# Value pages of a paged attention cache in 2 KB pieces on every eighth partition, two page groups to a double slot

## The chip, the cores and the metric

The kernel runs on one core of a Trainium2 chip. The time is device microseconds of one execution; the times given are those of several runs, and the profile is one more execution, taken by the hardware profiler.

## The reference: what is computed

One decoder layer for two request groups that share all weights: a prompt of 256 tokens, and 8 sequences of 8 new tokens each (64 rows) with 2,048 cached positions behind them. Model width is 1,024, so 320 rows go through everything: a SwiGLU feed-forward (width 2,816), a mixer, a second SwiGLU feed-forward, each with a layer norm behind it and scales and shifts from a condition vector.

The mixer has an attention half (8 heads of 64) and a convolution half (512 channels, 31 taps). For the 8 sequences the attention reads a paged cache. A page holds 128 positions of all 8 heads, as (head, position, 64) in float32: 256 KB of keys and 256 KB of values. Each sequence has 16 pages, in the order of a page table; together they are 32 MB of keys and 32 MB of values. Two pages make a block of 256 positions. Each query picks the three blocks of eight whose key sums score highest, and the softmax runs over those blocks and the new tokens, with a penalty per head that grows with distance. All pages are read, and blocks that were not picked are masked:

```
scores = q . k * scale - slope[head] * (q_pos - k_pos)      (all 2,048 positions)
gate   = q . mean(k of a block)      ->  the 3 highest blocks of 8
p      = softmax over picked blocks and own new tokens
out    = sum over positions of p * v
```

## The kernel before, in words

All five engines have their own hand-written instruction stream, tied by semaphores. SP issues nearly all loads in one fixed order; ACT issues a few of them. The order of the program is: feed-forward 1, the input projection of the mixer, the cached attention, the output projection, feed-forward 2. The weights are loaded in pieces of 1 KB per partition and row (`cols`), 1 MB at a time. At the very start SP also loads the tokens into `xrow`: `x_prompt` as 4 KB pieces on all 128 partitions (1 MB, line 484), and right behind it `x_sample` as 4 KB pieces on partitions 0 to 63 (256 KB, line 485).

**Chunks, slots, order.** The cached attention works on four pairs of sequences, j = 0 to 3. A pair has 32 pages. Four pages form a chunk of 1 MB, so a pair has eight key chunks and eight value chunks (k = 0 to 7; k 0 to 3 are the first sequence's, 4 to 7 the second's). The 64 chunks have numbers, `kvi`, and are loaded in this order: keys of pair 0, keys 1, values 0, keys 2, values 1, keys 3, values 2, values 3. They land in a ring of eight slots (`kv_slot`), each 128 partitions by 2,048 floats. The slots lie two by two: slots 0 to 3 are the tensor `raw`, 4 and 5 are `araw`, 6 and 7 are `kvw`. A chunk may be loaded when the chunk before it in its slot is used up (`kv_before`; the loop over `kvi` in the SP block). For keys this is the semaphore `kt_ready` (both halves turned), for values it is `v_used`. The last eight value chunks take slots 0 to 5, 2 and 3, since `kvw` takes the first two parts of the output weights `w_out` by then; SP issues those two loads behind value chunk 3 of pair 3, once the last two value chunks of pair 2 are used.

**How a page lands.** `load_pages` issues one DMA per page, four per chunk (x = 0 to 3). A key page covers all 128 partitions with 2 KB each. A value page x goes to partitions x, x + 4, x + 8 and so on, 32 of them, and on each come eight pieces of 1 KB (one per head, four positions each). The four pages of a chunk together fill all 128 partitions of one slot. For pairs 0 to 2 SP issues the pages x = 0, 1, 2 of each value chunk, and ACT issues x = 3 (`last_page` in `keys_low`), between its copies of the next pair's keys. For pair 3 SP issues all four.

**Keys.** For each key chunk PE turns the pages with 16 transposes (`turn_keys`, line 1865), ACT copies one half out of PSUM to `kT` (line 973) and DVE the other (line 1369), and PE multiplies with the queries (`scores`, line 1890). DVE then adds the distance term and takes sums and maxima per block (`score_chunk`).

**Values.** `pair_probs` turns the softmax numerators. `pair_values` (line 1960) takes chunk after chunk: it waits until the chunk has landed (`raw_wait`), does 8 products with the turned numerators as weights, and raises `v_used` by 1. The small steps of the next pair's softmax (`gate_sum`, `max_swap`, `prob_sum`), and in the last pairs those of the group norm and of the output projection, are called between chunks by the table `between`. Value chunks of pair j - 1 are used after the keys of pair j.

Of the kernel before, what the change touches and what calls it, by code (L numbers as in the profile page):

```python
# [72 lines left out]
def constants():  # L73
# [12 lines left out]

    col = np.arange(P)
    wide = np.arange(4 * P)
    c[:, C_POS:C_POS + 4 * P] = (wide // P % 2 * P + wide % P // 4 * 4 + 2 * (wide // 256))[None, :]

    h, r, t = p // 16, p // 8 % 2, p % 8
    m = 2.0 ** (-(h + 1.0))
# [152 lines left out]
def build(nc, i, o):  # L245
    es = ExitStack()
    with es:
# [96 lines left out]
        def kv_raw(kvi):  # L344

            k = kv_slot(kvi)
            return raw[:, k, :] if k < RING else (araw, kvw)[k // 2 - 2][:, k % 2, :]

        def kT_view(k, half):

            return kT[:, k % 2, 1024 * half:1024 * half + 1024].rearrange("p (x n q) -> p x q n", x=4, q=2)

        def bank_keys(half):

# [83 lines left out]
        def load_pages(eng, cache, kvi, page, xs=range(4)):  # L438

            slot = kv_raw(kvi)  # L440
            for x in xs:
                src = i["cache_" + cache][0][bass.ds(page[2 * x], 1)]
                if cache == "k":
                    eng.dma_start(slot[:, 512 * x:512 * x + 512], src.rearrange("a h (g r) d -> (a h g) (r d)", r=8)).then_inc(kv_in[kv_slot(kvi)], 16)
                else:
                    eng.dma_start(slot[x:P:4, :].rearrange("p (h f) -> p h f", h=NH),
                                  src.rearrange("a h (g r) d -> g (a h) (r d)", r=4)).then_inc(kv_in[kv_slot(kvi)], 16)


        @block.sync  # L450
        def _(sp):
# [98 lines left out]
            for kvi in range(KVN):  # L550
# [2 lines left out]
                    store_keys()  # L553
                if k % 4 == 0:
                    numbers = page_numbers(2 * j + k // 4)
                before = kv_before(kvi)
                if before is not None:
                    cache_b, jb, kb = kv_chunk(before)
                    sp.wait_ge(*((kt_ready, 2 * (8 * jb + kb + 1)) if cache_b == "k" else (v_used, 8 * jb + kb + 1)))
# [132 lines left out]
        def _(act):  # L692
# [264 lines left out]
            def keys_low(j, between={}):  # L957

                def last_page(k, page):

                    kvi = values_at(j - 1, k)
                    act.wait_ge(kt_ready, 2 * (8 * j + k + 1))
                    load_pages(act, "v", kvi, page[8 * (k % 4 // 2) + k % 2:], range(3, 4))

                numbers = None
                for k in range(8):
                    n = 8 * j + k
                    if j and k % 4 == 1:
                        numbers = page_numbers(2 * (j - 1) + k // 4, mybir.EngineType.Activation)
                    act.wait_ge(kt_ready, 2 * n + 1)  # L970
                    if n >= 2:
                        act.wait_ge(k_used, n - 1)
                    act.copy(kT_view(k, 0), bank_keys(0)).then_inc(kt_low, 1)  # L973
                    if n in ACT_HIGH:
                        act.wait_ge(kt_ready, 2 * n + 2)
                        act.wait_ge(kt_high, n)
                        act.copy(kT_view(k, 1), bank_keys(1)).then_inc(kt_high, 1)
                    if j and k:
                        last_page(k - 1, numbers)
                    if k in between:  # L980
                        between[k]()
                if j:
                    last_page(7, numbers)
# [549 lines left out]
        def _(pe):  # L1533
# [334 lines left out]
            def scores(j, k):  # L1868
# [9 lines left out]
                if k % 2 == 0:  # L1878
# [3 lines left out]
                        pe.wait_ge(s_evac, g + 3)  # L1882
                    elif j:
                        pe.wait_ge(pt_evac, 5 * j)
                keys = kT[:, k % 2, :].rearrange("p (i x h n) -> p i x h n", i=2, x=4, h=NH)
                for e in range(2):
                    for g4 in range(NHP):
                        h = 2 * g4 + e
                        out = bank[QG * g4:QG * g4 + QG, 4 + g % 2, :].rearrange("p (i c n x) -> p i c x n", i=2, c=2, x=4)[:, :, k % 2]
                        ins = pe.matmul(out, qb[:, 2 * j + k // 4, h, :], keys[:, :, :, h, :], start=e == 0, stop=e == 1)  # L1890
                ins.then_inc(k_used, 1)

# [37 lines left out]
            def pair_probs(j):  # L1930
# [4 lines left out]
                for r in range(4):  # L1935
                    if r >= 2:
                        pe.wait_ge(pt_evac, 5 * j + r - 1)
                    for x in range(4):
                        at = 512 * (r % 2) + 256 * (x % 2) + 128 * (x // 2)
                        ins = pe.transpose(bank[:, 4 + r % 2, P * x:P * x + P], s[:, r // 2, at:at + P], ident)  # L1940
                    ins.then_inc(pt_ready, 1)
                pe.wait_ge(ri_ready, j + 1)
# [4 lines left out]
            def pair_values(j, between):  # L1947


                if j:  # L1950
                    pe.wait_ge(av_evac, j)
                for k in range(8):
                    c, b2 = k % 4, k // 4
                    kvi = values_at(j, k)
                    raw_wait(kvi)
                    values = kv_raw(kvi).rearrange("p (h f) -> p h f", h=NH)
                    for i_ in range(2):
                        at = P * (8 * b2 + 2 * c + i_)
                        for g4 in range(NHP):
                            ins = pe.matmul(bank[QG * g4:QG * g4 + QG, 7, 256 * b2:256 * b2 + 256].rearrange("p (e f) -> p e f", e=2),  # L1960
                                            pT[:, at + QG * g4:at + QG * g4 + QG], values[:, 2 * g4:2 * g4 + 2, P * i_:P * i_ + P],
                                            start=(c == 0 and i_ == 0), stop=False)
                    ins.then_inc(v_used, 1)
                    if k in between:
                        between[k]()
                    if c == 3:

                        for g4 in range(NHP):
                            diagonal = bank[QG * g4:QG * g4 + QG, 7, 256 * b2:256 * b2 + 256].rearrange("p (a d) -> p a d", a=4)[:, 0:4:3, :]
# [65 lines left out]
                products(first[2 * u:2 * u + 2], m_parts(MIX_ORDER[c0:c1]), lambda n: pe.wait_ge(ml_ready, 16 + c0 + n + 1),  # L2035
                         start=c0 == 0, stop=False)

            pair_values(3, {2: group_scales, 5: lambda: conv_half(0, 0, NCC), 6: lambda: conv_half(1, 0, 2)})
            conv_half(1, 2, 3)
            attn_turn(3)  # L2040
            conv_half(1, 3, NCC)
# [74 lines left out]
```

## Time and profile before

| | |
|---|---|
| median of 3 runs | 912.44 us (907.31 to 916.94) |
| the profiled execution | 915.39 us |
| its span in the trace | 913.6 us |
| its mean granted clock of TensorE | 0.968 |
| PE busy | 848.8 us (93%) |
| DVE / ACT / POOL busy | 457.4 / 352.0 / 269.3 us |
| data moved by DMA | 197.44 MB, 216 GB/s over the span |
| chain that ended last | PE 73%, DVE 9%, DMA 6%, ACT 5% |

PE is the busiest engine over the whole program, since the three feed-forward and projection stages are nearly all PE. The cached attention is another stage with other limits. It lies between 430 and 628 us of the span: keys of pair 0 from 430, keys 1 from 458, values 0 from 492, keys 2 from 509, values 1 from 540, keys 3 from 558, values 2 from 583, values 3 from 603 to 627. Busy shares of the whole span say little about it; the rows below are of that stage.

The column for DMA in the windows view is the mean busy share of the 16 DMA engines, and can exceed 1 a little because packets overlap. Times of a load are from its issue to its landing.

### The profile page before, as it was taken

The page shows a single profiled execution, that of the slowest core. Times are in us where ns is not written, and L with a number is a line of the kernel's source. Part 1 is how long each engine was busy: PE and PEld are TensorE (multiplying, and loading weights), DVE is VectorE, ACT ScalarE, POOL GpSimd, SP SyncE. Part 2 cuts the span into 40 slices and gives each one's busy share as a digit, 9 for nine tenths or more (in the row PEclk, how much of TensorE's full clock was granted, in tenths as well). Part 3 has the DMA queues.
Part 4 walks back from the last instruction along what each step waited for, and adds up shares of the span by engine and source line. Part 5 has one row for each costly group of instructions (what it writes and reads, how often), then busy time and mean ns, then how long its engine had stood idle before and what let it go on. Part 6 is the DMA issues. An engine that isn't in the chain of part 4 may idle for free.

```text
span 913.6 us, 17049 instructions
## 1 busy us (share of the span) xinstructions
PE 848.8 (93%) x6754; PEld 749.9 (82%) x6754; DVE 457.4 (50%) x710; ACT 352.0 (39%) x500; POOL 269.3 (29%) x326
## 2 busy tenths in 40 slices
PE   5699999999899998999987879769989999999997
PEld 3498888988899988988764656538889999999996
DVE  1544333433243465844686776834853444444353
ACT  2323233233222458455443314273573433342230
POOL 2020000000010222999999999701200000000120
PEclk9599999999999999999998899999999999999998
DMA  9966776879956453416997999998424544644421
GB/s 301 353 203 222 249 237 222 261 227 308 325 173 219 140 160 122 155 47 203 357 306 256 366 332 377 348 349 281 141 67 131 172 139 138 187 151 129 162 70 58
DMA packets 182129, 197.44 MB, mean 216 GB/s; under 512 B 11907, under 2 KB 163705, under 8 KB 182053
## 3 DMA queue, kind: packets, MB, share of 16 engines
q1 hardware_dynamic: 175149, 190.04, 64.3%
q10 hardware_dynamic: 6624, 6.33, 2.1%
q8 instruction: 46, 0.75, 0.4%
q0 software_dynamic: 288, 0.14, 0.1%
q14 instruction: 22, 0.18, 0.1%
HBM read 193.67 MB, written 3.17 MB: 215 GB/s over the span
## 4 chain that ended last, share of the span: by engine, by line
PE 73%; DVE 9%; DMA 6%; ACT 5%; issue 3%; SPq 2%; POOL 1%; DVEq 0%; ACTq 0%; POOLq 0%
PE bank L1597 18%; PE bank L1599 17%; PE bank L1598 17%; PE bank L1865 5%; DMA raw<-in_ffn_wg 3%; PE bank L1573 3%; PE bank L1890 3%; DVE kT L1369 1%; PE bank L1960 1%; DMA xrow<-in_x_sample 1%; PE bank L1562 1%; DVE wlo L1083 1%; DMA raw<-in_ffn_wu 1%; ACT uT L832 1%; DMA araw<-in_cache_v 1%
## 5 line engine op out<-in xcount | busy, mean ns | idle before, releaser
L1083 DVE TENSOR_TENSOR wlo<-raw,whi 128x2048 fp32r<-128x2048 f32 (+1 forms) x80 | 183.7, 2296 | 242.2 <-ACT whi L710 241.9
L1597 PE MATMUL bank<-mh,whi 128*128 128x320 f32 x816 | 258.2, 316 | 4.7 <-ACT yT L915 2.3
L1599 PE MATMUL bank<-mh,wlo 128*128 128x320 f32 x816 | 252.8, 310 | 0.0
L1598 PE MATMUL bank<-ml,whi 128*128 128x320 f32 x816 | 252.7, 310 | 0.0
L710 ACT CAST whi<-raw 128x2048 fp32r<-128x2048 f32 (+1 forms) x80 | 149.2, 1866 | 231.6 <-PE bank L1599 159.1
L1597 PEld LDWEIGHTS bank<-mh,whi 128*128 128x128 f32 x816 | 154.0, 189 | 15.5 <-issue 15.5
L1598 PEld LDWEIGHTS bank<-ml,whi 128*128 128x128 f32 x816 | 154.1, 189 | 0.1
L1599 PEld LDWEIGHTS bank<-mh,wlo 128*128 128x128 f32 x816 | 153.8, 189 | 0.0
L1597 PE MATMUL bank<-hh,whi 128*128 128x320 f32 x352 | 111.1, 316 | 0.0
L1598 PE MATMUL bank<-hl,whi 128*128 128x320 f32 x352 | 109.4, 311 | 0.0
L1599 PE MATMUL bank<-hh,wlo 128*128 128x320 f32 x352 | 109.4, 311 | 0.0
L677 POOL TENSOR_SCALAR tmp<-cbuf,dwT 128x256 f32<-128x256 f32 x90 | 89.3, 992 | 0.0
L684 POOL TENSOR_TENSOR yT<-yT,tmp 128x320 f32<-128x320 f32 x90 | 84.0, 933 | 7.5
L610 POOL TENSOR_TENSOR tmp<-yT 128x320 f32<-128x320 f32 x3 | 4.6, 1521 | 239.8 <-DVE yT L1137 239.8
L1597 PEld LDWEIGHTS bank<-hh,whi 128*128 128x128 f32 x352 | 66.7, 189 | 2.6 <-issue 2.5
L1598 PEld LDWEIGHTS bank<-hl,whi 128*128 128x128 f32 x352 | 66.8, 190 | 0.2
L1599 PEld LDWEIGHTS bank<-hh,wlo 128*128 128x128 f32 x352 | 66.7, 190 | 0.0
L650 POOL TENSOR_TENSOR fold_g<-adaT,par 128x72 f32<-128x72 f32 x2 | 0.6, 318 | 200.6 <-DVE adaT L1103 200.6
L973 ACT COPY kT<-bank 128x1024 f32<-128x1024 f32 x32 | 35.6, 1112 | 56.7 <-PE bank L1865 56.7
L768 ACT ACTIVATE tmp<-bank 128x320 f32<-128x320 f32 x44 | 19.2, 439 | 94.9 <-PE bank L1599 88.6
L1159 DVE TENSOR_TENSOR tmp<-bank,tmp 128x320 f32<-128x320 f32 x44 | 21.4, 489 | 59.8 <-PE bank L1599 37.0
L1369 DVE COPY kT<-bank 128x1024 f32<-128x1024 f32 x30 | 36.6, 1221 | 27.9 <-PE bank L1865 27.8
(269 smaller groups left out, 1146.7 us busy)
## 6 DMA issues: line engine op xcount, KB each, us to landing
araw<-in_w_ada SPq DMA_DIRECT2D x28, 1024.0 KB, 5.2
raw<-in_ffn_wg SPq DMA_DIRECT2D x22, 1024.0 KB, 7.1
raw<-in_ffn_wu SPq DMA_DIRECT2D x22, 1024.0 KB, 7.2
raw<-in_ffn_wd SPq DMA_DIRECT2D x16, 1024.0 KB, 5.3
raw<-in_cache_k SPq DMA_DIRECT2D x64, 256.0 KB, 4.3
raw<-in_cache_v SPq DMA_DIRECT2D x60, 256.0 KB, 5.6
raw<-in_w_in SPq DMA_DIRECT2D x10, 1024.0 KB, 5.2
raw<-in_w_ada SPq DMA_DIRECT2D x8, 1024.0 KB, 12.3
```

The source lines that it names most:

```text
L677: pool.tensor_scalar(to[:, 0:SEQ], cbuf[:, c, k:k + SEQ], w, *more)
L684: pool.tensor_tensor(acc_c, acc_c, to, ALU.add).then_inc(conv_ready if last else pool_step, 1)
L710: act.copy(wh(slot_w(phase, u))[:, 0:size], landed(phase, u)[:, 0:size]).then_inc(w_hi, 1)
L973: act.copy(kT_view(k, 0), bank_keys(0)).then_inc(kt_low, 1)
L1083: dve.tensor_tensor(wl(slot_w(phase, u))[:, 0:size], landed(phase, u)[:, 0:size], wh(slot_w(phase, u))[:, 0:size].bitcast(F32), ALU.subtra ...
L1369: dve.tensor_copy(kT_view(k, 1), bank_keys(1)).then_inc(kt_high, 1)
L1573: ins = pe.matmul(bank[g:g + QG, b + a_ % 2, 0:UC], cT[:, kk, :], src[:, UC * kk:UC * kk + UC], start=kk < 4, stop=kk >= 4)
L1597: pe.matmul(bank[:, b, 0:T], wh(slot)[:, c], h_, start=(start and n == 0), stop=False)
L1598: pe.matmul(bank[:, b, 0:T], wh(slot)[:, c], l_, start=False, stop=False)
L1599: ins = pe.matmul(bank[:, b, 0:T], wl(slot)[:, c], h_, start=False, stop=(stop and n == len(parts) - 1))
L1865: ins = pe.transpose(bank[:, 2 * half + x // 2, to:to + P], slot[:, at:at + P], ident)
L1890: ins = pe.matmul(out, qb[:, 2 * j + k // 4, h, :], keys[:, :, :, h, :], start=e == 0, stop=e == 1)
```

## The change

A value page now goes to 16 partitions instead of 32: every eighth one, with eight pieces of 2 KB on each (one per head, eight positions each). The chunk with an even number takes the partitions whose number leaves 0 to 3 when divided by 8, the chunk with the odd number those that leave 4 to 7. On these partitions a page spreads over both slots of a two-slot tensor: heads 0 to 3 in the first slot, 4 to 7 in the second (`kv_pair`). So two chunks, eight pages, share a double slot. Three waits follow from this. SP loads an even value chunk only when both slots are free (`kvi | 1`). ACT does the same for its page. PE waits for both chunks of a double slot, then does 16 products of the same size where it had twice 8, and raises `v_used` by 2; the steps of `between` come after both.

The position that a partition stands for is thereby changed, and the scores have to have the same order before they are turned. So the copies to `kT` and the score products write and read in another order (`kT_view`, `keys`, `out`), and the table of distances (`C_POS`) follows. The key loads are not changed.

```diff
-    c[:, C_POS:C_POS + 4 * P] = (wide // P % 2 * P + wide % P // 4 * 4 + 2 * (wide // 256))[None, :]
+    c[:, C_POS:C_POS + 4 * P] = (wide % 8 // 4 * P + wide % P // 8 * 8 + wide // P % 2 * 4 + wide // (2 * P) * 2)[None, :]
...
+        def kv_pair(kvi):
+
+            k = kv_slot(kvi) // 2 * 2
+            pair = raw[:, k:k + 2, :] if k < RING else (araw, kvw)[k // 2 - 2][:, :, :]
+            return pair.rearrange("p a f -> p (a f)").rearrange("p (h f) -> p h f", h=NH)
+
         def kT_view(k, half):
-            return kT[:, k % 2, 1024 * half:1024 * half + 1024].rearrange("p (x n q) -> p x q n", x=4, q=2)
+            return kT[:, k % 2, 1024 * half:1024 * half + 1024].rearrange("p (q x n) -> p x q n", x=4, q=2)
...
                 else:
-                    eng.dma_start(slot[x:P:4, :].rearrange("p (h f) -> p h f", h=NH),
-                                  src.rearrange("a h (g r) d -> g (a h) (r d)", r=4)).then_inc(kv_in[kv_slot(kvi)], 16)
+                    eng.dma_start(kv_pair(kvi)[4 * (kvi % 2) + x:P:8],
+                                  src.rearrange("a h (g r) d -> g (a h) (r d)", r=8)).then_inc(kv_in[kv_slot(kvi)], 16)
...
-                before = kv_before(kvi)
+                before = kv_before(kvi if cache == "k" else kvi | 1)
...
-                    act.wait_ge(kt_ready, 2 * (8 * j + k + 1))
+                    act.wait_ge(kt_ready, 2 * (8 * j + (k | 1) + 1))
...
-                keys = kT[:, k % 2, :].rearrange("p (i x h n) -> p i x h n", i=2, x=4, h=NH)
+                keys = kT[:, k % 2, :].rearrange("p (a x h n) -> p a x h n", a=4, x=4, h=NH)
...
-                        out = bank[QG * g4:QG * g4 + QG, 4 + g % 2, :].rearrange("p (i c n x) -> p i c x n", i=2, c=2, x=4)[:, :, k % 2]
+                        out = bank[QG * g4:QG * g4 + QG, 4 + g % 2, :].rearrange("p (a n c x) -> p a c x n", a=4, c=2, x=4)[:, :, k % 2]
...
-                        at = 512 * (r % 2) + 256 * (x % 2) + 128 * (x // 2)
+                        at = 512 * (r % 2) + 128 * x
...
-                for k in range(8):
+                for k in range(0, 8, 2):
                     c, b2 = k % 4, k // 4
                     kvi = values_at(j, k)
                     raw_wait(kvi)
-                    values = kv_raw(kvi).rearrange("p (h f) -> p h f", h=NH)
-                    for i_ in range(2):
-                        at = P * (8 * b2 + 2 * c + i_)
+                    raw_wait(kvi + 1)
+                    values = kv_pair(kvi)
+                    for a in range(4):
+                        at = P * (8 * b2 + 2 * c + a)
+                        f = HD * (4 * (a % 2) + 2 * (a // 2))
...
-                    ins.then_inc(v_used, 1)
-                    if k in between:
-                        between[k]()
-                    if c == 3:
+                    ins.then_inc(v_used, 2)
+                    for n in (k, k + 1):
+                        if n in between:
+                            between[n]()
+                    if c == 2:
...
-            pair_values(3, {2: group_scales, 5: lambda: conv_half(0, 0, NCC), 6: lambda: conv_half(1, 0, 2)})
+            pair_values(3, {2: group_scales, 4: lambda: conv_half(0, 0, NCC), 5: lambda: conv_half(1, 0, 2)})
```

Two places of the instruction order show it. The first is SP's queue at the value chunks 1 and 2 of pair 1, behind the stores of the convolution state. Before:

```order
L540 DMA out_conv_sample_new<-tmp 8x512 x7
L446 ISA [waits kt_ready]
L446 DMA raw<-in_cache_v 32x8x256
L446 ISA
L446 DMA raw<-in_cache_v 32x8x256
L446 ISA
L446 DMA raw<-in_cache_v 32x8x256
L446 ISA [waits kt_ready]
L446 DMA raw<-in_cache_v 32x8x256
```

Now:

```order
L546 DMA out_conv_sample_new<-tmp 8x512 x7
L452 ISA [waits kt_ready]
L452 DMA raw<-in_cache_v 16x8x512
L452 ISA
L452 DMA raw<-in_cache_v 16x8x512
L452 ISA
L452 DMA raw<-in_cache_v 16x8x512
L452 ISA [waits kt_ready]
L452 DMA raw<-in_cache_v 16x8x512
```

Number and order of the loads stay; each has 16 by 8 pieces of 512 floats where it had 32 by 8 of 256. The same holds on ACT's queue.

The second place is PE in `pair_values(3)`: products with the value chunks (`raw,pT` and `araw,pT`), those of the group norm (`tmp,con`), and those with the new tokens (`vsam,po`). Before:

```order
L1960 MATMUL bank<-raw,pT 32x256 [waits kv_in1]
L1960 MATMUL bank<-raw,pT 32x256 x7
L1960 MATMUL bank<-raw,pT 32x256 [waits kv_in2]
L1960 MATMUL bank<-raw,pT 32x256 x7
L2024 MATMUL bank<-tmp,con 128x320 [waits gr_ready]
L2024 MATMUL bank<-tmp,con 128x320 x3
L1960 MATMUL bank<-raw,pT 32x256 [waits kv_in3]
L1960 MATMUL bank<-raw,pT 32x256 x7
L1970 MATMUL bank<-vsam,po 32x2x64 x4
L1960 MATMUL bank<-araw,pT 32x256 [waits kv_in4]
```

Now:

```order
L1968 MATMUL bank<-raw,pT 32x256 [waits kv_in0,kv_in1,av_evac,pt_evac]
L1968 MATMUL bank<-raw,pT 32x256 x15
L1968 MATMUL bank<-raw,pT 32x256 [waits kv_in3,kv_in2]
L1968 MATMUL bank<-raw,pT 32x256 x15
L2033 MATMUL bank<-tmp,con 128x320 [waits gr_ready]
L2033 MATMUL bank<-tmp,con 128x320 x3
L1979 MATMUL bank<-vsam,po 32x2x64 x4
L1968 MATMUL bank<-araw,pT 32x256 [waits kv_in5,kv_in4]
```

One wait for two chunks stands where each chunk had its own, and the group norm's products moved behind chunk 3.

## Rows read from the trace of the kernel before

**Rows 1.** The page, part 2: 40 equal slices of the span.
```profile
DMA  9966776879956453416997999998424544644421
GB/s 301 353 203 222 249 237 222 261 227 308 325 173 219 140 160 122 155 47 203 357 306 256 366 332 377 348 349 281 141 67 131 172 139 138 187 151 129 162 70 58
```

**Rows 2.** Windows by attention step: stretch and length, busy per engine, clock, DMA.
```profile
458.00:486.00 28.00, 25.13 (x274) 18.00 (x265) 23.89 (x44) 13.17 (x14) 27.00 (x36) 1.00 0.94 308
486.00:508.00 22.00, 17.11 (x201) 10.47 (x202) 13.70 (x40) 7.26 (x14) 21.33 (x27) 0.84 0.76 268
508.00:539.00 31.00, 26.78 (x279) 19.92 (x281) 22.41 (x33) 10.04 (x12) 29.81 (x41) 0.89 1.00 338
539.00:558.00 19.00, 14.42 (x192) 8.04 (x188) 14.10 (x39) 5.12 (x10) 18.42 (x22) 0.91 1.05 372
558.00:583.00 25.00, 23.55 (x281) 17.78 (x281) 16.93 (x19) 9.62 (x11) 24.08 (x34) 1.00 1.09 360
583.00:602.00 19.00, 15.11 (x196) 8.69 (x188) 10.17 (x32) 6.32 (x13) 5.99 (x9) 1.00 1.10 348
602.00:628.00 26.00, 19.36 (x212) 12.53 (x210) 10.45 (x11) 13.24 (x19) 0.00 (x0) 0.87 1.10 347
```

**Rows 3.** Timeline of PE: start, length, line, operation, count, idle time before.
```profile
460.82 2.02 PE L1865 MATMUL bank<-con,raw 128*128 128x128 f32 x16 [0.40 <-ACT kT L973]
...
552.75 1.93 PE L1960 MATMUL bank<-kvw,pT 128*32 128x256 f32 x32
...
590.41 0.38 PE L1919 MATMUL bank<-nmax,con 128*128 128x2 f32 x2 [1.70 <-DVE nmax L1408]
...
596.60 1.93 PE L1960 MATMUL bank<-kvw,pT 128*32 128x256 f32 x32
...
613.05 1.63 PE L1960 MATMUL bank<-araw,pT 128*32 128x256 f32 x16 [3.74 <-DMA araw<-in_cache_v]
616.03 1.93 PE L1960 MATMUL bank<-araw,pT 128*32 128x256 f32 x16 [1.35 <-DMA araw<-in_cache_v]
...
626.63 0.42 PE L1970 MATMUL bank<-vsam,po 64*32 64x128 f32 x8
```

**Rows 4.** Timeline of SP's queue from the last waits for `v_used` on.
```profile
598.21 3.03 SPq L573 DMA_DIRECT2D kvw<-in_w_out  x2
602.44 7.25 SPq L446 DMA_DIRECT2D araw<-in_cache_v  x8
609.88 6.75 SPq L446 DMA_DIRECT2D raw<-in_cache_v  x8
```

**Rows 5.** Windows again: key loads, value loads, `x_prompt`, `x_sample`.
```profile
446.00:458.00 12.00, 10.96 (x145) 7.95 (x147) 9.44 (x10) 4.12 (x4) 11.58 (x16) 1.00 1.04 386
588.00:608.00 20.00, 16.52 (x226) 9.57 (x220) 8.71 (x21) 10.13 (x19) 1.15 (x2) 1.00 1.10 348
...
9.00:12.30 3.30, 2.85 (x29) 0.70 (x19) 0.00 (x0) 0.37 (x1) 0.00 (x0) 1.00 1.05 382
12.40:13.60 1.20, 1.20 (x7) 0.96 (x6) 0.27 (x2) 0.31 (x1) 0.00 (x0) 1.00 1.01 189
```

**Rows 6.** DMA issues: tensor, queue, count, KB each, median us to landing.
```profile
raw<-in_cache_v SPq DMA_DIRECT2D x60, 256.0 KB, 5.6
raw<-in_cache_v ACTq DMA_DIRECT2D x12, 256.0 KB, 6.0
```

**Rows 7.** Key loads of SP (issue time, time to landing), then value loads.
```profile
L444 SPq DMA_DIRECT2D raw<-in_cache_k x64: 331/333/1358, 375.3 to 550.4; - x64
DMA to landing us min/median/max: 2.5/4.6/9.5
...
L446 SPq DMA_DIRECT2D raw<-in_cache_v x60: 602/602/1311, 460.6 to 616.0; - x60
```

**Rows 8.** Score products and value products: ns min, median, max.
```profile
L1890 PE MATMUL bank<-kT,qb x512: 376/379/636, 434.8 to 583.3; 128*32 128x256 f32 x171
L1960 PE MATMUL bank<-kvw,pT x96: 379/379/403, 503.2 to 598.2; 128*32 128x256 f32 x96
```

More of the change, by code:

```diff
@@ L1955, in pair_values @@
                     raw_wait(kvi)
-                    values = kv_raw(kvi).rearrange("p (h f) -> p h f", h=NH)
-                    for i_ in range(2):
-                        at = P * (8 * b2 + 2 * c + i_)
+                    raw_wait(kvi + 1)
[3 more added lines that the diff above has]
+                        f = HD * (4 * (a % 2) + 2 * (a // 2))
                         for g4 in range(NHP):
                             ins = pe.matmul(bank[QG * g4:QG * g4 + QG, 7, 256 * b2:256 * b2 + 256].rearrange("p (e f) -> p e f", e=2),
-                                            pT[:, at + QG * g4:at + QG * g4 + QG], values[:, 2 * g4:2 * g4 + 2, P * i_:P * i_ + P],
-                                            start=(c == 0 and i_ == 0), stop=False)
-                    ins.then_inc(v_used, 1)
-                    if k in between:
-                        between[k]()
-                    if c == 3:
+                                            pT[:, at + QG * g4:at + QG * g4 + QG], values[:, 2 * g4:2 * g4 + 2, f:f + P],
+                                            start=(c == 0 and a == 0), stop=False)
+                    ins.then_inc(v_used, 2)
[3 more added lines that the diff above has]
+                    if c == 2:
                         for g4 in range(NHP):
```

## The prediction

> **What bounds the kernel now.** I began with the slices of the page [rows 1]: in slices 25 to 28 (571 to 640 us) the DMA engines are busy without a break, which they are hardly anywhere else after the start. The windows by attention step [rows 2] say where: from 486 us on, the DMA share climbs from 0.76 over 1.00 and 1.05 to 1.09 and 1.10, and it stays at 1.10 to the end of the attention at 627 us. PE in the same rows has gaps in every stage. The timeline of PE [rows 3] shows what ends them in the last stage: two waits for `cache_v`, 3.74 us before chunk 4 of pair 3 and 1.35 us before chunk 5. No earlier value chunk is waited for there. So the loads are the limit at the end of the attention alone, and just behind the other limits before it: from 458 to 558 us loads keep pace because slots come free at the pace of the keys (eight key chunks in 25 us, 558 to 583).
>
> How fast a load goes depends on its form [rows 5]. Key loads (2 KB pieces, 128 partitions) move 386 GB/s at a share of 1.04, value loads (1 KB pieces) 348 at 1.10. A chunk is 1.049 MB: 2.72 us as keys, 3.01 us as values. Two more rows stand in the same group because of the change. `x_prompt`, on 128 partitions, moves at 382 GB/s. `x_sample`, right behind it, goes to partitions 0 to 63 only, and then all engines together move 189 GB/s at a share of 1.01: as busy as ever, and half as fast.
>
> **The change part by part.** *Larger pieces.* Same number of loads, 16x8 pieces of 2 KB for 32x8 of 1 KB. Upper bound of the rate: the key row, 386 GB/s, 2.72 us a chunk. Issuing on SP: a value load holds SP for 602 ns, a key load with the same number of pieces as the new one for 331 to 333 [rows 7], so about 0.27 us less for each load; SP is ahead of the DMA engines in the last stages, and I count nothing.
>
> *Fewer partitions at a time.* This is what decides. Until now the four pages of a chunk fill all 128 partitions, and even one page touches every group of four. Now the four pages of an even chunk, 1 MB, all go to partitions 0 to 3 of every eight, and the next 1 MB to 4 to 7. For the length of a chunk, half of the partitions receive nothing. The only row of this trace in which half of the partitions receive nothing is `x_sample`, and it has half the rate. Lower bound: 189 GB/s, 5.55 us a chunk. That row is only 1.2 us long and cut at both ends; half of the key rate is 193, or 5.43 us, and I use that where SP alone loads (pair 3). I take this end of the range rather than 386 because in what the two differ the new loads are like `x_sample`: today's value pages land on few partitions too (32) and are fast, so it is not their number but that a whole half stays idle. The pages from ACT's queue soften it for pairs 0 to 2: they are 2 of the 8 pages of a double slot. If such a page is of the other half than the one SP's queue is at, both halves receive and the rate is whole. At best 4 of 8 pages then move at 386 and 4 at 193: 8.15 us for two chunks, 4.08 each; at worst 5.43. I take the middle, 4.75.
>
> The Trainium skill gives the mechanism ("SBUF — State Buffer", "Door 1: The DMA port swizzle"): a partition's DMA port follows from bits 2 to 4 and bit 6 of its number, there are 16 ports, and bandwidth depends on how many a transfer reaches. Partitions 0 to 63 reach 8 ports; so does every eighth partition with its three neighbours. The trace agrees with that on `x_sample`. The page gives 196 GB/s for such a transfer of 1 MiB and 218 as its limit; by an estimate from these, a chunk would be 5.35 or 4.81 us, and the sum below, with all 32 value chunks at that, would end 61 or 43 us later than now.
>
> *What that does to the end.* I string the loads together. Value pair 0 can start when key chunk 1 of pair 1 is turned, 460.82 + 2.02 = 462.84 us [rows 3]. From there SP's queue holds 32 value chunks, 16 key chunks (pairs 2 and 3) and, before the last four value chunks, 2 MB of `w_out` (1 KB pieces, 2 x 3.01). Landing lags by 1.8 us (least time to landing of a key load 2.5, less 0.68 us for its 256 KB [rows 7]), and the last two chunks need 1.93 + 0.42 us of PE [rows 3]. With c us per value chunk the attention ends at 462.84 + 1.8 + 16 x 2.72 + 6.0 + 2.35 + 32c = **516.5 + 32c**, if the DMA engines never run dry. It ends now at 627.05. So c decides from 3.45 us (304 GB/s) on; below, the present limits hold. With 24 x 4.75 + 8 x 5.43 = 157.4 the end is 673.9: **+46.9 us**. I went through it stage by stage for dry spells: value pair 0 lands until about 503 (464.6 + 8 x 4.75), within the stage of 486 to 508 in which it is used [rows 2]; the keys of pair 2 follow until 524 and are used from 509 on at 3 us each, so nothing is lost yet. Values 1 land until about 562, where their products end at 555 now; values 2 until about 622, where they end at 598.5 now [rows 3]; values 3 last. From values 1 on, slots are free before the queue reaches them, so the stream has no gap, and each stage waits for its last double slot.
>
> *Double slots.* SP waits for two slots, so the first chunk of each two is released up to one key chunk (3 us) or one value chunk (1 us) later; PE waits for two chunks. Both are hidden while the queue has a backlog, and that is so from values 1 on. If the loads were fast (cover gone), the cost would be under 3 us at the end: there chunks 6 and 7 of pair 3 are issued from 609.88 on [rows 4], after both slots are free. `max_swap` and the group norm step now follow chunk 3 instead of 2, one chunk of PE's work (1 us) being moved; before `max_swap` PE waits 1.70 us for DVE now [rows 3], which covers it.
>
> *Other order of keys.* Same instructions and sizes. ACT and DVE copy the same 1,024 elements. The score products now write every eighth float of PSUM instead of every fourth. Bounds: nothing, and twice their time, 32 chunks x 1.0 us. The row says nothing: with a step of four they take 379 ns at the median, as the value products do that write without a step [rows 8]. The Trainium skill ("SBUF — State Buffer", the note on cachelines) says that any non-contiguous PSUM access slows matmuls significantly; this trace does not show it.
>
> *Behind the attention.* `w_out` parts 2 and 3 and the first weights of feed-forward 2 follow in SP's queue, 3 us each, as before; they move with the rest. I count 0.
>
> Sum: 915.4 (profiled execution) + 46.9 = 962.3. That execution lies 3 us above the median of 912.4, so against the median 912.4 + 46.9 = **959 us**.
>
> **The rivals.** (1) *Half a rate, as forecast*, c between 4.2 and 5.6: 936 to 981 by the same line. Chance 0.78. Against it: the row is short, and its neighbour's 1 KB packets share it.
>
> (2) *The halves overlap.* The queue holds the even and the odd chunk one behind the other. If engines drift apart by a chunk, one writes the lower half while another writes the upper, and 2 KB pieces run at up to 386 GB/s. From 304 GB/s on this rival decides. Then the two waits go: w_out and the last four chunks start at 598.2 [rows 4], and 6.0 + 10.9 + 1.8 + 2.35 us later it is 619.3, 7.7 us before now: 905 us, **faster**. For it: today's pages of 32 partitions run without loss, at 347 to 348 GB/s also where `w_out` comes between them (602 to 628) [rows 2]. Against: every engine gets the same chunk at the same time, and nothing in a queue pushes them apart by 64 KB. Chance 0.13.
>
> (3) *Somewhere between*, 290 to 310 GB/s, or the gain eaten by the double slots: within 1% of now. Chance 0.05.
>
> (4) *PE's order costs*: the score products double, and 4 x 8 us come in at the four key stages; with fast loads 912 + 32 - 8 = 936. Chance 0.04. That the pieces stay 1 KB can be left out: the order shows 16x8x512.
>
> **The numbers.** Forecast 959. The range has to hold 8 in 10: nearly all of (1), (4), and the upper part of (3), so 914 to 980. About 1% (9 us) is what can be told from no change. Faster 0.13, same 0.05, slower 0.82.
>
> **What would show it.** Right: windows in which value loads alone run (in values 3 above all) at about 190 to 220 GB/s with a DMA share near 1; value loads with landing times well above today's 5.6 to 6.0 us [rows 6]; PE waits for `cache_v` in values 1, 2 and 3, growing, 10 us and more in the last; key windows still at 386; the score products at 379 ns; the lengths before 458 us and after the attention unchanged. Wrong: value loads at over 300 GB/s, or waits of PE at keys instead of values. Were the rate half but the end early, the step that failed would be the string of loads, at a dry spell or an overlap with ACT's pages that I mis-sized.

## The result, and the profile after

| | before | after |
|---|---|---|
| median of 6 runs each | 914.41 us (907.31 to 916.94) | **965.12 us** (959.64 to 972.52) |
| ratio | 1 | **1.0566** (95%: 1.0536 to 1.0596) |
| the profiled execution | 915.39 us | 965.69 us |
| its span, mean granted clock | 913.6 us, 0.968 | 963.9 us, 0.937 |
| first score product to last value product | 192.2 us | 243.3 us |
| from there to the end of the span | 286.6 us | 286.9 us |

The change makes the kernel 5.7% slower. The forecast was 959 us, 46.9 us more than the 912.4 known then; measured are 965.1 us, 50.7 more than the 914.4 of six runs, and inside the range of 914 to 980.

The last two lines of the table say where. The stretch from the first score product to the last value product is called the attention below. Its ends are the first `bank<-kT,qb` and the last `bank<-vsam,po` product in PE's timeline (start, length, ..., count, and in brackets the idle time before and what ended it). Before the first one stood at

```profile
434.83 1.07 PE L1890 MATMUL bank<-kT,qb 128*32 128x256 f32 x16
```

and the last as in [rows 3] (626.63 + 0.42 = 627.05). After:

```profile
433.64 1.07 PE L1896 MATMUL bank<-kT,qb 128*32 128x256 f32 x16
...
504.57 3.64 PE L1968 MATMUL bank<-kvw,pT 128*32 128x256 f32 x32 [2.40 <-DMA kvw<-in_cache_v]
...
565.42 3.64 PE L1968 MATMUL bank<-kvw,pT 128*32 128x256 f32 x32 [2.94 <-DMA kvw<-in_cache_v]
...
626.63 3.64 PE L1968 MATMUL bank<-kvw,pT 128*32 128x256 f32 x32 [4.43 <-DMA kvw<-in_cache_v]
636.29 1.93 PE L1968 MATMUL bank<-raw,pT 128*32 128x256 f32 x32 [1.13 <-DMA raw<-in_cache_v]
646.33 3.64 PE L1968 MATMUL bank<-raw,pT 128*32 128x256 f32 x32 [8.10 <-DMA raw<-in_cache_v]
663.94 3.64 PE L1968 MATMUL bank<-araw,pT 128*32 128x256 f32 x32 [12.01 <-DMA araw<-in_cache_v]
674.70 1.93 PE L1968 MATMUL bank<-raw,pT 128*32 128x256 f32 x32 [0.89 <-DMA raw<-in_cache_v]
676.56 0.42 PE L1979 MATMUL bank<-vsam,po 64*32 64x128 f32 x8
```

The attention is 51.1 us longer, the program outside it as long as before. What PE waits for is in its groups of the stretch from 457 to 690 us (count | busy, mean ns | idle before and what ended it):

```profile
L1968 PE MATMUL bank<-raw,pT 128*32 128x256 f32 x288 | 25.9, 521 | 29.0 <-DMA raw<-in_cache_v 29.0
L1968 PE MATMUL bank<-araw,pT 128*32 128x256 f32 x128 | 11.2, 507 | 14.7 <-DMA araw<-in_cache_v 14.7
L1968 PE MATMUL bank<-kvw,pT 128*32 128x256 f32 x96 | 10.9, 633 | 9.8 <-DMA kvw<-in_cache_v 9.8
```

53.5 us of waiting for `cache_v`, where [rows 3] had 3.74 + 1.35 = 5.1. That difference, 48.4 us, is nearly the whole loss. The windows by attention step answer to [rows 2] (keys 1, values 0, keys 2, values 1, keys 3, values 2, values 3). The last two rows are a stretch of key loads alone and one of value loads alone, and answer to the key and the value row of [rows 5]:

```profile
457.00:486.00 29.00, 25.10 (x274) 18.00 (x266) 24.73 (x45) 12.21 (x14) 28.00 (x36) 1.00 0.94 210
486.00:512.00 26.00, 16.90 (x218) 10.34 (x218) 17.93 (x50) 7.77 (x16) 25.16 (x32) 0.87 1.06 276
512.00:538.00 26.00, 24.16 (x280) 17.68 (x276) 18.78 (x22) 8.57 (x10) 24.97 (x35) 1.00 1.06 304
538.00:573.00 35.00, 20.42 (x184) 10.93 (x184) 14.00 (x40) 5.51 (x11) 33.83 (x44) 0.61 1.06 258
573.00:599.00 26.00, 24.08 (x278) 17.63 (x274) 17.30 (x18) 8.52 (x10) 14.24 (x20) 1.00 1.06 303
599.00:635.00 36.00, 21.95 (x200) 11.77 (x200) 9.51 (x32) 6.95 (x15) 0.00 (x0) 0.72 1.07 220
635.00:677.00 42.00, 19.87 (x195) 12.45 (x191) 10.39 (x11) 11.73 (x15) 0.00 (x0) 0.67 1.08 233
505.00:520.00 15.00, 14.27 (x150) 9.98 (x146) 11.53 (x24) 6.37 (x11) 14.47 (x20) 0.87 1.06 387
625.00:640.00 15.00, 10.23 (x114) 5.59 (x114) 2.15 (x1) 5.26 (x10) 0.00 (x0) 0.78 1.07 216
```

Read the last two numbers of each row, the busy share of the DMA engines and the GB/s. From 486 us on the engines are busy throughout, and where value loads run alone they move 216 GB/s where it was 348. Key loads still move 387. The number before them is the granted clock: in values 1 to 3, where PE idles most, its mean is 0.61, 0.72 and 0.67, and the 32 instructions of a double slot's products take 3.64 us in many places where they take 1.93 at full clock. That is an effect and not a cause: the slow products left no gap in the loads (shares of 1.06 to 1.08), and behind the last slow double slot, at 663.94 us, PE still had to wait 0.89 us for the last load.

The loads by themselves, first the page (KB, median us to landing), then the issue times (ns) of SP's value loads to `raw`, and the landings of all value loads, against [rows 6, 7]:

```profile
raw<-in_cache_k SPq DMA_DIRECT2D x64, 256.0 KB, 8.0
raw<-in_cache_v SPq DMA_DIRECT2D x60, 256.0 KB, 15.9
raw<-in_cache_v ACTq DMA_DIRECT2D x12, 256.0 KB, 8.4
...
L452 SPq DMA_DIRECT2D raw<-in_cache_v x60: 557/620/2752, 462.0 to 656.7; - x60
DMA to landing us min/median/max: 3.9/15.5/22.5
L1896 PE MATMUL bank<-kT,qb x512: 377/379/404, 433.6 to 598.3; 128*32 128x256 f32 x171
```

A value load from SP takes 15.9 us to land, not 5.6. The score products (last row) are as before [rows 8].

### The profile page after: what moved, and what is told of

Its sections match the earlier page's. It is cut to its first block, busy times and chain, and to the rows that moved or that the text cites. A ratio compares the mean times of both kernels' runs of the same rounds, so it can differ in the third digit from the quotient of the medians.

```text
span 963.9 us, 17065 instructions
## 1 busy us (share of the span) xinstructions
PE 861.0 (89%) x6754; PEld 754.3 (78%) x6754; DVE 458.3 (48%) x710; ACT 347.9 (36%) x500; POOL 269.1 (28%) x326
## 4 chain that ended last, share of the span: by engine, by line
PE 64%; SPq 14%; DMA 7%; DVE 5%; ACT 4%; issue 4%; POOL 0%; DVEq 0%; ACTq 0%; POOLq 0%
PE bank L1603 18%; PE bank L1605 17%; PE bank L1604 17%; SPq L452 7%; SPq L450 4%; DMA raw<-in_cache_v 4%; PE bank L1579 3%; PE bank L1871 2%; DMA raw<-in_w_ada 2%; PE bank L1568 1%; DMA raw<-in_ffn_wg 1%; DVE wlo L1089 1%; SPq L439 1%; PE bank L1896 1%; DMA raw<-in_ffn_wu 1%
## 5 line engine op out<-in xcount | busy, mean ns | idle before, releaser
L979 ACT COPY kT<-bank 128x1024 f32<-128x1024 f32 x32 | 32.4, 1013 | 54.3 <-PE bank L1871 54.3
L1968 PE MATMUL bank<-raw,pT 128*32 128x256 f32 x288 | 25.9, 521 | 29.0 <-DMA raw<-in_cache_v 29.0
## 6 DMA issues: line engine op xcount, KB each, us to landing
raw<-in_cache_v SPq DMA_DIRECT2D x60, 256.0 KB, 15.9
```

## Experiments

Each edit is against the changed kernel unless it says "before". Ratios are to the kernel before, run on the same chip (medians 912.6 to 914.1 us); they come from all runs and not from the two medians alone. "Attention" is the stretch of the table above in the profiled execution; 192.2 us before, 243.3 with the change. The executions differ in when the attention starts (431.8 to 436.7 us), which that measure leaves out. It comes from one execution of each kernel, and where that one lies far from its median this is said.

**1. The old landing, everything else as changed.**

```diff
-                    eng.dma_start(kv_pair(kvi)[4 * (kvi % 2) + x:P:8], ... r=8)
+                    eng.dma_start(slot[x:P:4, :].rearrange("p (h f) -> p h f", h=NH), ... r=4)
```

> The changed kernel with all of its waits, double slots and its order of keys and scores, but each value page landing as before: 32 partitions, every fourth one, eight 1 KB pieces, in its own slot. (The values then stand at other positions than the numerators expect; only the time counts.) Theory A (only the landing costs, since for the length of a chunk half of the DMA ports stand idle): value loads back at 348 GB/s, no wait of PE for cache_v beyond about 5 us in all, time 908 to 918. Rival B (the double slots cost: PE and SP wait for two chunks at once): the time stays well above 920, with waits for cache_v or v_used in values 1 to 3. Rival C (the new order of scores costs PE): key stages longer than 25 us.

Measured 919.35 us, ratio 1.0038 (1.0011 to 1.0066); attention 194.9 us. The landing is 46 us by the medians and 48 by the attention, of 51. Double slots and the new order of keys and scores together are 0.1 to 0.7%. The value loads are back at the old rate, as theory A has it:

```profile
580.00:600.00 20.00, 16.57 (x223) 9.58 (x216) 13.66 (x37) 5.59 (x11) 9.21 (x13) 1.00 1.10 349
```

Two things it had too low: PE waits 11.2 us for `cache_v` (2.20 and 8.97 us, both in values 3) and not 5, and the time lies a little above 908 to 918.

**2. Pages of the even and the odd chunk alternate in SP's queue.**

```diff
...
+                elif k % 2 == 0:
+                    for x in xs:
+                        for c in range(2):
+                            load_pages(sp, cache, kvi + c, numbers[8 * (k % 4 // 2) + c:], range(x, x + 1))
```

> The changed kernel, complete, with one thing else: SP issues the pages of the even and the odd chunk of a double slot in turn (even page 0, odd page 0, even page 1, ...) instead of four and four. Theory A with engines that can fall half a period apart once that is only one page, 16 KB per DMA engine: value loads at 300 to 386 GB/s and 903 to 918 us. Theory A with engines in step, whatever the order: each page alone has two engines on a port, so 218 GB/s as now and 960 to 970 us. Rival D (the 2 KB pieces with 32 KB between them in memory are slow to read): no change either, 960 to 970; e3 and e4 tell these apart.

Measured 949.16 us, 1.0366 (1.0325 to 1.0408); attention 229.3 us, in an execution of 954.19 us, 5.0 above its median. Window in values 2, value loads alone:

```profile
590.00:610.00 20.00, 10.49 (x106) 6.08 (x110) 10.74 (x30) 1.01 (x1) 0.00 (x0) 0.67 1.07 253
```

With 256 KB of one half and then 256 KB of the other the queue moves some 250 GB/s, a sixth more than 216, far from 387. Order within the queue matters, so it is not the page's form alone. The time lies in neither of the two ranges: the halves overlap, but only in a small part.

**3 and 4. Two loads of equal shape on 64 partitions: every other one, or one half of the array.** They have two pieces of 2 KB on each of 64 partitions, and put the values elsewhere (`kv_both` is the double slot as partition, slot, float).

```diff
+                    eng.dma_start(kv_both(kvi)[kvi % 2:P:2, :, 512 * x:512 * x + 512], ... c=2)
```

```diff
+                    eng.dma_start(kv_both(kvi)[64 * (kvi % 2):64 * (kvi % 2) + 64, :, 512 * x:512 * x + 512], ... c=2)
```

> The changed kernel, but a value page lands on 64 partitions with 4 KB each (2 KB in either slot, read in sequence from memory): the even chunk's pages on partitions 0, 2, 4, ..., the odd chunk's on 1, 3, 5, .... (Values then stand elsewhere; only the time counts.) For the length of a chunk half of the partitions receive nothing, as in the change, but all 16 ports of the skill's map are reached. Theory A by ports: 380 GB/s or so, 905 to 915 us. Theory A as my prediction worded it by rows (half of the partitions idle means half the rate): about 200 GB/s and 955 to 975 us.

> As the run with even and odd partitions, with one thing else: the even chunk's pages land on partitions 0 to 63, the odd chunk's on 64 to 127. Again half of the partitions idle, and here only 8 of the 16 ports of the skill's map are reached. Theory A by ports: 218 GB/s, 955 to 975 us, like the change. Rival D (the order in which memory is read is what costs; here it is read in sequence): 340 to 386 GB/s, 905 to 918 us.

Every other partition: 917.23 us, 1.0024 (1.0002 to 1.0047), attention 195.5 us. One half: 970.47 us, 1.0616 (1.0578 to 1.0654), attention 244.2 us (an execution of 966.84 us, 3.6 below its median). A window of the first in values 3, where the loads of its last four value chunks run all but alone,

```profile
610.00:620.00 10.00, 2.74 (x28) 1.55 (x32) 6.23 (x7) 8.22 (x11) 0.00 (x0) 0.62 1.05 386
```

and of the second in values 1:

```profile
540.00:560.00 20.00, 8.92 (x76) 4.36 (x76) 8.65 (x27) 1.64 (x3) 19.33 (x25) 0.63 1.07 214
```

This pair decides what "half" means. In both, half of the partitions receive nothing for a chunk, with the same bytes, pieces and number of loads. One runs at 386 GB/s, the other at 214. How many partitions are idle is not what counts, but which. And since the second reads each page in sequence and is slow all the same, the order in which memory is read (rival D) is not the cause. Theory A by ports was right for the slow case; for the fast one it was 2 us too hopeful (905 to 915), see experiment 7.

The Trainium skill has the rule ("SBUF — State Buffer", "Door 1: The DMA port swizzle"): bits 2 to 4 and 6 of the partition number choose one of 16 ports. Even partitions reach all 16; 0 to 63 reach 8, and so do the changed kernel's sets. The rates agree with it: 386 with all 16 ports, 214 and 216 with 8, just under the page's limit of 218 GB/s for 8 ports.

**5. As 2, with half pages of 128 KB alternating.**

```diff
+                    for hs in halves:
+                        eng.dma_start(kv_pair(kvi)[4 * (kvi % 2) + x:P:8, 4 * hs:4 * hs + 4], ...
```

> As the run that alternates pages of the even and the odd chunk, but each value page is loaded by two DMAs of four heads each, and these alternate: 8 KB per DMA engine on one half of the ports, then 8 KB on the other, as often as the pages of 32 partitions did before the change. Twice as many value loads are issued. In-step theory (two engines on one port stay in step unless the period is short enough that they fall apart): rate between that of the whole pages in turn (218 to 274 GB/s) and 386, time 915 to 945. Rival (a load of 16 partitions is slow by itself, in whatever order): 945 to 965, as with whole pages. Issuing could also become the limit, at 12 DMAs for 6.

Measured 971.95 us, 1.0652 (1.0608 to 1.0697), slower than both theories had it. Its time does not answer its question, for issuing became the limit. A window in values 2 with a backlog, one in values 3 without, and the issue times:

```profile
600.00:610.00 10.00, 6.26 (x72) 4.12 (x76) 5.51 (x8) 1.01 (x1) 0.00 (x0) 0.90 1.07 281
630.00:650.00 20.00, 9.69 (x110) 5.42 (x102) 2.15 (x1) 5.26 (x10) 0.00 (x0) 0.76 0.56 167
...
L453 SPq DMA_DIRECT2D raw<-in_cache_v x120: 557/557/1488, 462.6 to 678.5; - x120
```

In the second window the DMA share is 0.56: the engines starve, since SP needs 557 ns for 128 KB just as for 256 KB, 235 GB/s at the very most. The first window does say something. There the loads issued before have piled up, the share is 1.07, and value loads alone move 281 GB/s, where whole pages in turn moved 253 and whole chunks 216. Finer steps within a queue bring the halves closer together; whether still finer ones would reach 386 stays open.

**6. Even value chunks on SP's queue, odd ones on ACT's.**

```diff
-                load_pages(sp, cache, kvi, numbers[8 * (k % 4 // 2) + k % 2:], range(3 if cache == "v" and j < 3 else 4))
+                if cache == "k" or k % 2 == 0:
+                    load_pages(sp, cache, kvi, numbers[8 * (k % 4 // 2) + k % 2:])
...
+                    if k % 2:
+                        load_pages(act, "v", kvi, page[8 * (k % 4 // 2) + 1:])
...
```

For pair 3, where ACT issued nothing, it now issues the odd chunks too.

> The changed kernel, complete, with even value chunks issued by SP and odd ones by ACT, so that two queues hold work for opposite halves at the same time (in the change ACT issues one page of four, and none in values 3). Theory A with overlap of two queues (this is what made me take 4.75 us a chunk rather than 5.43 for pairs 0 to 2): value rates of 300 to 386 GB/s in all stages and 912 to 930 us. Rival (queues don't overlap on the ports, engines take both queues' work in step): 218 to 250 GB/s, 955 to 970 us. ACT is held for 4 x 0.56 us per odd chunk, which may cost up to 5 us in the key stages.

Measured 930.02 us, 1.0199 (1.0157 to 1.0241); attention 207.1 us. Windows in values 0, 1 and 2:

```profile
470.00:480.00 10.00, 9.16 (x98) 6.64 (x98) 9.81 (x13) 5.58 (x8) 9.66 (x12) 1.00 1.06 219
540.00:550.00 10.00, 7.33 (x108) 3.79 (x100) 8.78 (x27) 0.29 (x1) 9.67 (x12) 0.90 1.06 351
590.00:610.00 20.00, 14.90 (x198) 8.66 (x190) 6.62 (x27) 7.47 (x16) 0.00 (x0) 1.00 1.06 351
```

The same loads to the same partitions move 351 GB/s once each half has its queue and both have a backlog. Then the packets of either queue take half of the engines' time (52% and 52% from 540 to 545 us). Early in values 0 and 1 they come in turn instead: from 470 to 475 us ACT's queue has 74% and SP's 31%, and the rate is that of one half, though both queues hold loads. Of the 51 us, 36 come back. Bytes, pieces and partitions are those of the change; besides the queue, the odd chunks of pair 3 no longer stand behind `w_out`, and no run takes that apart. The Trainium skill says that two transfers to opposite halves serialize, with 6% gained ("SBUF — State Buffer", "Can I just issue two DMAs to hit both halves?"). In one queue the trace agrees for whole chunks (216 GB/s), and so it does early in values 0; in two queues with a backlog this run measured over 60% more.

**7. Before, with values loaded in the form of the keys** (2 KB pieces, 128 partitions; the values stand elsewhere).

```diff
-                    eng.dma_start(slot[x:P:4, :].rearrange("p (h f) -> p h f", h=NH), ... r=4)
+                    eng.dma_start(slot[:, 512 * x:512 * x + 512], src.rearrange("a h (g r) d -> (a h g) (r d)", r=8))
```

> The kernel before, with its single slots and waits, but value pages loaded in the form of key pages: 128 partitions, one 2 KB piece each. (The values stand elsewhere; only the time counts.) It measures what fast value loads are worth without double slots. My second rival said 7.7 us faster (905 for 912): 902 to 910. If instead another limit stands right behind the loads, as the run with even and odd partitions suggests (917 us at full rate), 910 to 915.

Measured 910.43 us, 0.9972 (0.9939 to 1.0004); attention 186.2 us, 6.0 less, in an execution of 905.93 us, 4.5 below its median.

```profile
560.00:590.00 30.00, 25.38 (x312) 17.51 (x313) 23.58 (x44) 6.91 (x8) 25.28 (x35) 1.00 1.05 386
```

It shows about the most that faster value loads can give: key and value loads both at 386 GB/s in this window, two waits of 0.51 and 1.64 us left, and about 3 us of the median, with no change inside the interval.

**8. Before, with `w_out` loaded later**, behind all but two of the last value chunks.

```diff
-                if kvi == KVN - RING - 1:
+                if kvi == KVN - 3:
```

> The kernel before, complete, with one thing else: SP issues the first two parts of the output weights behind value chunk 5 of pair 3 instead of behind chunk 3. PE waited 3.74 and 1.35 us for value chunks 4 and 5 at 613 and 616 us, while 2 MB of weights lay ahead of them in the queue (6 us). If these waits are on the path: 2 to 5 us faster. If the end of the stream alone counts (the same bytes come in by the same time): within 1 us of before. Slower by 1 to 3 us if the products with the output weights, which now come later, were what filled PE's time.

Measured 917.64 us, 1.0046 (1.0018 to 1.0074), so slower by 2 to 7 us and none of the three cases. In the profiled execution, the longest of ten (922.11 us), the attention takes 195.5 us (3.3 more) and what follows it 288.6 us (2.1 more). PE's two waits for value chunks are gone. In their place stands one for the products with `w_out` (`mh,whi`), which before filled the time between chunks 5 and 6:

```profile
610.56 2.05 PE L1960 MATMUL bank<-araw,pT 128*32 128x256 f32 x32
621.42 0.61 PE L1610 MATMUL bank<-mh,whi 128*128 128x320 f32 x1 [8.80 <-DVE ml L1469]
```

ACT, which turns the loaded `w_out` into `whi`, had waited 10.01 us for that load, and DVE's `wlo` and `ml` came behind it. Whichever of the two loads comes last, PE waits for it; taking 2 MB from ahead of the last chunks is no remedy here.

**9. Changed, with all value pages on SP's queue.**

```diff
-                load_pages(sp, cache, kvi, numbers[8 * (k % 4 // 2) + k % 2:], range(3 if cache == "v" and j < 3 else 4))
+                load_pages(sp, cache, kvi, numbers[8 * (k % 4 // 2) + k % 2:], range(4))
```

> The changed kernel, complete, with all four pages of every value chunk issued by SP; ACT issues none. If ACT's pages do overlap with SP's on the other half of the ports (the changed kernel moved 240 to 250 GB/s while both queues held value pages, 216 to 220 otherwise), all value windows now stand at 216 to 220 and the end comes 3 to 10 us later: 968 to 975 us. If the higher rates had another cause, they stay, and so does the time, 962 to 967.

Measured 965.38 us, 1.0600 (1.0547 to 1.0653); attention 244.5 us. Windows in values 0, 1 and 2:

```profile
470.00:500.00 30.00, 22.05 (x285) 14.41 (x283) 22.07 (x44) 11.09 (x17) 29.00 (x37) 1.00 1.07 212
525.00:540.00 15.00, 13.69 (x184) 9.66 (x183) 11.46 (x13) 3.84 (x4) 14.42 (x21) 1.00 1.07 225
605.00:630.00 25.00, 11.02 (x96) 6.21 (x100) 4.49 (x10) 3.92 (x8) 0.00 (x0) 0.70 1.07 219
```

The second window still has key loads in its first three microseconds. In the change the same stretches moved 221, 246 and 221 GB/s. So the rates fell, as the first branch of the expectation has it, and the time stayed, as the second has it: the attention is 1.2 us longer, and the intervals of the two ratios overlap. Why a little more rate gives so little time, no run shows.

**10. Before, with the double slots alone**: the pairs of waits, `v_used` by twos and the table `between` of the change, with the old landing and order.

```diff
-                before = kv_before(kvi)
+                before = kv_before(kvi if cache == "k" else kvi | 1)
...
-                for k in range(8):
+                for k in range(0, 8, 2):
...
-                    ins.then_inc(v_used, 1)
+                    ins.then_inc(v_used, 2)
```

> The kernel before, complete, landing and order of scores untouched (32 partitions, 1 KB pieces), with only the waits of the double slots: SP and ACT load value chunks when both slots of two are free, PE waits for both chunks, frees both at once, and the steps between chunks move as in the change. The run with the old landing in the changed kernel took 0.4% more than before (0.1 to 0.7). If that came from the double slots, this one takes the same: 914 to 919, ratio 1.002 to 1.007. If it came from the order of the scores and key copies, it takes 913, as before.

Measured 917.40 us, 1.0057 (1.0033 to 1.0081), 3 to 7 us. PE now waits once for chunks 4 and 5 of pair 3:

```profile
613.05 3.46 PE L1961 MATMUL bank<-araw,pT 128*32 128x256 f32 x32 [7.06 <-DMA araw<-in_cache_v]
```

7.06 us for the 5.09 of [rows 3]. This execution (913.14 us) is the shortest of nine, 4.3 us below the median, and its attention is 192.4 us, 0.2 us longer, so it does not show where the 3 to 7 us are spent. The interval of run 1 overlaps this one; what run 1 adds to it, the order of keys and scores, has no cost that can be measured.

## Why the prediction was right, and which sizes were off

**What bounds it: right.** The loads limited the end of the attention alone; making them slower moved that end, and experiment 7 shows how little was to be had from making them faster. One reading was loose: the slices of [rows 1] stand at 9 not only from 571 us on but from 502, so the engines were busy, though not yet the limit, well before.

**The half rate: right in direction and mechanism, too coarse in its words.** I took the rate of `x_sample` [rows 5] because "a whole half stays idle". Experiment 3 leaves half of the partitions idle and loses nothing; what must be idle is half of the ports. The size was 12% off: 193 GB/s predicted, 216 measured in the windows with value loads alone, so 4.86 us a chunk and not 5.43. The row of 1.2 us was too short for a rate. The estimate that I worked out from the Trainium skill's limit of 218 GB/s gave +43 us; the windows agree with the 218, and the loss was some 8 us larger.

**The overlap with ACT's pages: wrong.** I gave pairs 0 to 2 a chunk time of 4.75 us because a quarter of the pages come by another queue. Experiment 9 takes them away, and its attention is 1.2 us longer. So nearly all of the 24 x (5.43 - 4.75) = 16.3 us of forecast gain did not exist. It was covered by the error before it, 32 x (5.43 - 4.86) = 18.2 us the other way: the sum of 157.4 us stands against 32 x 4.86 = 155.5, and came out near by luck, through two errors that cancel.

**The string of loads: right, 5 us short.** It said 673.9 us for the end, the trace has 676.98. I expected no dry spell, and the share is 1.06 to 1.08 in every window from 486 us on. Values 1 to 3 each wait for their last double slot; values 0 do too, by 2.40 us, which I had at nothing. With 4.86 us a chunk the line 516.5 + 32c gives 672.0 for the end, and 2.35 less, 669.7, for the last landing. The products of the last double slot start when that load has landed, at 674.70 us. So the 5 us that are left lie in the stream of loads and not in PE's waits for pairs of chunks. Which loads took longer than their rows say, no run takes apart.

**Double slots: under-sized.** "Under 3 us" was said for fast loads; experiment 10, with the loads of before, measures 3 to 7. Its one visible wait is at the end of pair 3 behind `w_out`, but at chunks 4 and 5, which are now waited for together, and not at 6 and 7. With the slow loads of the change the cost is hidden, as I said: there the last landing sets the end.

**Issue on SP: wrong, at no cost.** I expected a value load to hold SP for the 332 ns of a key load; it is 557 at the least, and 620 at the median of the row above, instead of 602. In front of a queue with a backlog nothing hangs on it.

**Order of keys and scores, behind the attention: right**, 379 ns and 286.9 us against 286.6.

**Rival 2 failed twice.** Even and odd chunks in one queue moved 216 GB/s and not up to 386. That fits its counter-argument, that nothing in a queue drives the engines apart; experiments 2 and 5 show that smaller steps change it in part. And its 905 us was too good. Experiment 3 has the changed kernel's double slots and the fast loads and comes to 917, with one wait of 8.46 us at chunk 4:

```profile
617.26 3.64 PE L1973 MATMUL bank<-araw,pT 128*32 128x256 f32 x32 [8.46 <-DMA araw<-in_cache_v]
```

Its step of 7.7 us for fast loads is about what experiment 7 shows in the attention (6.0), but the median has 3.

**Rival 4** (score products twice as long) is excluded by the row of 379 ns.

No version beat the kernel before. The only one below it, experiment 7, is within its uncertainty and does not lay the values out as the products need them.

## What to carry to other kernels

Judge a load by the set of partitions that the queue writes over some hundreds of KB, not by the size of its pieces: larger pieces moved 386 GB/s against 348, and with half of the ports idle it was 216. Where a layout forces such loads, put the two halves on two queues that hold equal work at the same time; here that brought back 36 of 51 us, and still lost to the old layout. And ask first what the faster load could give: here it was about 3 us, not told apart from nothing, against 50 at risk. When you read a rate from a window, look up first which loads land in it: keys and values alternate every 20 to 40 us here, and a window of keys shows 387 GB/s whatever the values do.

## What the runs showed of the hardware that was not expected

- **Issue time follows the form, not the number of pieces.** Shortest issue on SP: 128 x 512 floats 332 ns, 64 x 2 x 512 537 to 542, 16 x 8 x 512 and 16 x 4 x 512 both 557, 32 x 8 x 256 602. All with a third dimension are above 530; half the pieces saved nothing.
- **Opposite halves overlap by how they stand in the queues.** 216 GB/s by chunks in one queue, 253 by pages, 281 by half pages, 351 in two queues once both have a backlog.
- **ScalarE's copy to `kT` got faster** by 0.10 us. It now writes in sequence and not every second float, and it goes with that alone: 1013 ns in experiment 1 (new order, old landing), 1112 in experiment 10 (old order, double slots). VectorE's did not change (1.23 and 1.22 us). Before and after:

```profile
L973 ACT COPY kT<-bank x32: 1076/1114/1138, 431.1 to 579.7; 128x1024 f32<-128x1024 f32 x32
```

```profile
L979 ACT COPY kT<-bank x32: 1012/1013/1020, 429.9 to 594.6; 128x1024 f32<-128x1024 f32 x32
```
